# Plain fp32 for the first weight pieces of a two-block transformer kernel, and another order of its opening loads

## The reference

```
c_act = silu(c)                                   # c: 2048 numbers
mod   = c_act @ w_ada + b_ada                     # w_ada: 2048 x 12288
sh_m, sc_m, gt_m, sh_f, sc_f, gt_f = split(mod, 6)
h     = rmsnorm(x, pre_mix_norm) * (1 + sc_m) + sh_m
proj  = h @ w_in                                  # w_in: 2048 x 8208
```

## Time and profile before

| | |
|---|---|
| median of three executions | 2838.78 us |
| profiled execution: span, first to last instruction | 2835.2 us |
| the same execution's time outside its span | not shown by the profile; median minus span is 3.6 us |
| TensorE busy | 95% of the span, granted clock 0.980 of 2.4 GHz |
| VectorE busy | 68% |
| ScalarE busy | 45% |
| DMA over the span | 578.42 MB, 204 GB/s |
| the chain that ended last | TensorE 83%, VectorE 8%, DMA 5%, issue 2%, ScalarE 1% |

### The profile page before, as it was taken

The page is one execution under the profiler, slowest core; times in us unless marked ns, Lnnn a source line. Parts: engine busy times, 40 slices in busy tenths (PEclk is TensorE's granted clock), DMA queues, the critical chain, the costliest instruction groups (busy, mean ns, idle before and its releaser), DMA issues.

```text
span 2835.2 us, 35190 instructions
## 1 busy us (share of the span) xinstructions
PE 2696.8 (95%) x12829; PEld 2244.1 (79%) x12829; DVE 1937.8 (68%) x2165; ACT 1261.8 (45%) x1423; POOL 22.7 (1%) x12
## 2 busy tenths in 40 slices
PE   3699999999799999999989999999999999999998
PEld 3578878777688888888868788888888888888886
DVE  7979796987856666666675657555557666666667
ACT  2253453554444444444445454444444444444444
POOL 0000000000000000000000000000000000000000
PEclk8799999999999999999999999999999999999999
DMA  9968666567566666666646446665556666666664
GB/s 354 340 213 252 218 219 217 174 195 264 184 219 219 203 219 208 214 217 205 218 137 193 127 148 199 201 198 181 194 169 203 189 188 187 190 186 188 188 187 154
DMA packets 281266, 578.42 MB, mean 204 GB/s; under 512 B 19642, under 2 KB 20308, under 8 KB 280020
## 3 DMA queue, kind: packets, MB, share of 16 engines
q1 hardware_dynamic: 279060, 572.95, 63.1%
q10 hardware_dynamic: 2112, 4.19, 0.4%
HBM read 574.98 MB, written 2.10 MB: 204 GB/s over the span
## 4 chain that ended last, share of the span: by engine, by line
PE 83%; DVE 8%; DMA 5%; issue 2%; ACT 1%; SPq 0%; ACTq 0%; DVEq 0%
PE bank L450 25%; PE bank L451 25%; PE bank L455 25%; PE bank L708 4%; PE bank L705 3%; DMA ada_raw<-in_w_ada 2%; DMA early<-in_w_ada 2%; DVE w_lo L440 2%; DVE acc L1848 1%; DVE acc_w L1848 1%; DVE gd_t L2203 1%; PE bank L1113 0%; DVE gd_t L1817 0%; ACT w_hi L435 0%; DVE at_t L1817 0%
## 5 line engine op out<-in xcount | busy, mean ns | idle before, releaser
L440 DVE TENSOR_TENSOR w_lo<-raw,w_hi 128x1024 fp32r<-128x1024 f32 x880 | 1074.2, 1228 | 629.9 <-ACT w_hi L435 627.6
L435 ACT ACTIVATE w_hi<-raw 128x1024 fp32r<-128x1024 f32 x880 | 930.6, 1059 | 1254.2 <-PE bank L455 1118.9
L450 PE MATMUL bank<-w_hi,op_a_hi 128*128 128x512 f32 x2272 | 904.8, 398 | 34.1 <-DVE op_a_lo L1817 31.9
L451 PE MATMUL bank<-w_hi,op_a_lo 128*128 128x512 f32 x2272 | 890.7, 392 | 0.0
L455 PE MATMUL bank<-w_lo,op_a_hi 128*128 128x512 f32 x2272 | 610.6, 391 | 5.0 <-DVE w_lo L440 5.0
L450 PEld LDWEIGHTS bank<-w_hi,op_a_hi 128*128 128x128 f32 x2272 | 430.6, 190 | 125.2 <-DVE op_a_lo L1817 32.6
L455 PEld LDWEIGHTS bank<-w_lo,op_a_hi 128*128 128x128 f32 x2272 | 428.5, 189 | 95.8 <-DVE w_lo L440 5.8
L451 PEld LDWEIGHTS bank<-w_hi,op_a_lo 128*128 128x128 f32 x2272 | 430.7, 190 | 86.7 <-issue 1.0
L450 PE MATMUL bank<-w_hi,hid_hi 128*128 128x512 f32 x832 | 326.5, 392 | 0.0
L451 PE MATMUL bank<-w_hi,hid_lo 128*128 128x512 f32 x832 | 323.9, 389 | 0.0
L455 PE MATMUL bank<-w_lo,hid_hi 128*128 128x512 f32 x832 | 222.7, 389 | 0.0
(11 more groups left out here) (240 smaller groups left out, 1875.3 us busy)
## 6 DMA issues: line engine op xcount, KB each, us to landing
raw<-in_w_in SPq DMA_DIRECT2D x264, 512.0 KB, 4.6
raw<-in_w_ff SPq DMA_DIRECT2D x256, 512.0 KB, 3.7
raw<-in_ffn_w_up SPq DMA_DIRECT2D x176, 512.0 KB, 4.1
ada_raw<-in_w_ada SPq DMA_DIRECT2D x96, 512.0 KB, 5.3
raw<-in_ffn_w_down SPq DMA_DIRECT2D x88, 512.0 KB, 4.7
early<-in_w_ada SPq DMA_DIRECT2D x26, 1024.0 KB, 12.4
raw<-in_w_out SPq DMA_DIRECT2D x32, 512.0 KB, 4.8
ada_raw_f<-in_w_ada SPq DMA_DIRECT2D x32, 512.0 KB, 4.7
```

The costliest lines, as they stand in the source:

```text
L435: nc.scalar.activation(w_hi[:, gj % RAW], raw[:, j % RAW], ACT.Copy).then_inc(hi_ready, 1)
L440: nc.vector.tensor_tensor(w_lo[:, gj % RAW], raw[:, j % RAW], w_hi[:, gj % RAW].bitcast(F32), ALU.subtract).then_inc(lo_ready, 1)
L450: nc.tensor.matmul(where[:, t], hi(kt + k, tok), w_hi[:, s, k], start=first and k == 0, stop=False)
L451: nc.tensor.matmul(where[:, t], lo(kt + k, tok), w_hi[:, s, k], start=False, stop=False)
```

## The change

- Pieces 0 to 14 and piece 18 (`WHOLE`) are no longer split. TensorE multiplies them as they are, in plain float32, with the unsplit operand `X_T`: four products of 128x512 per piece (`whole_piece`). Such a step waits for the piece's landing and for `h32_ready`, or, for the first two rows of a quarter, for a new counter `xt_half` that VectorE raises when half of the quarter is modulated. Pieces 15, 16, 17 and everything from 19 on are split as before; `rounded(n)` counts only the split ones.
- SP loads only the unit matrix of the constants (64 KB) at first, then c alone, then blocks 4 and 5, then all other row vectors (14), then the remaining blocks with nothing between them. After block 31 come four small reads for the delta rule and the attention (`a_log`, `dt_b`, `sink`, `ab_raw`) and the rest of the constants, under one counter `rest_landed`.
- x is issued by ScalarE, behind blocks 0 to 3 and after its exponential for c_act. ScalarE also issues pieces 0 to 19 (`load_in(act, ...)`): 0 to 3 after each `X_T` copy, 4 to 9 after the first rounding, 10 to 15 after the second, 16 to 19 after the third, with the splits of 15, 16 and 17 between them.
- VectorE sums three pairs before it norms x. In the second and third quarter, half a pair of the next quarter stands ahead of the modulation. The bounds of the HGRN2 group (`bounds_open`, `bounds_done`) are made around pair 4 instead of at the start. The last pair is summed block by block (`add_last`).
- The decay stages begin at step 20 instead of 18; the delta-rule stages begin where they did.

```
+WHOLE = tuple(range(15)) + (18,)
-EARLY_LOADS = {7: range(0, 4), 11: range(4, 8), 17: (8, 9), 19: (10, 11), 25: (12, 13), 27: (14, 15), 29: (16,), 31: (17, 18, 19)}
...
+        def whole_piece(pe, n, kt, where, first, last):
+            raw_landed(pe, 0, n)
+            if kt % 4:
+                pe.wait_ge(h32_ready, kt // 4 + 1)
+            else:
+                pe.wait_ge(xt_half, kt // 4 + 1)
+            for k in range(PK):
+                for t in range(NT):
+                    mm = nc.tensor.matmul(where[:, t], X_T[:, kt + k, t * P:(t + 1) * P], raw[:, n % RAW, k],
+                                          start=first and k == 0, stop=last and k == PK - 1)
+            mm.then_inc(w_used, 1)
...
+        def load_in(eng, n):
+            m = n - RAW
+            if m in WHOLE:
+                eng.wait_ge(w_used, m + 1)
+            elif m >= 0:
+                eng.wait_ge(lo_ready, rounded(m))
+            load(eng, 0, n, win_piece(n))
...
-            sp.dma_start(table[:], consts).then_inc(loaded, 16)
+            sp.dma_start(ident, consts[:, C_ID:C_ID + P]).then_inc(loaded, 16)
...
-            sp.dma_start(X[:], x_in).then_inc(x_landed, 16)
...
+                if n == 31:
...
+                    sp.dma_start(table[:, P:], consts[:, P:]).then_inc(rest_landed, 16)
...
 (ScalarE)
+            nc.scalar.dma_start(X[:], x_in).then_inc(x_landed, 16)
...
                 f(X_T[:, 4 * q:4 * q + 4].rearrange("p k n -> p (k n)"), flat(n), ACT.Copy, xt_ready)
+                load_in(act, q)
...
-            for q in range(4):
-                for n in EARLY_SPLITS[q]:
-                    split_hi(act, 0, n, 0, n)
-                round_early(q)
...
+            round_early(0)
+            for n in range(RAW, 10):
+                load_in(act, n)
+            round_early(1)
+            for n in range(10, 16):
+                load_in(act, n)
+            round_early(2)
+            for n in range(EARLY_DONE - RAW, EARLY_DONE):
+                if n - 1 not in WHOLE:
+                    split_hi(act, 0, n - 1, 0, n - 1)
+                load_in(act, n)
+            for n in range(EARLY_DONE - 1, EARLY_DONE + 1):
+                split_hi(act, 0, n, 0, n)
+            round_early(3)
+            act.wait_ge(rest_landed, 80)
...
 (VectorE)
             add_early(0)
+            add_early(1)
+            add_early(2)
             newton(0)
             scaled_rows()
...
+            for q in range(1, 4):
+                add_early(4 * q + 1)
+                early_low(q - 1)
+                add_early(4 * q + 2)
+                if q < 3:
+                    add_early(4 * q + 3)
+                    add_early(4 * q + 4, (0, 1))
+                    early_operand(q)
+                    add_early(4 * q + 4, (2, 3))
+                else:
+                    early_split(*(n for n in range(12, 18) if n not in WHOLE))
+                    add_last(15)
+                    early_operand(3)
```

176 lines of the change are left out of this document (77 added, 99 removed).

## The result

The changed kernel is slower, by 0.26%: 2846.8 us (median of 9 runs, 2842.8 to 2849.9) against 2839.3 for the kernel before, measured beside it (9 runs, 2833.6 to 2844.1). The ratio is 1.0026, with a 95% interval of 1.0017 to 1.0034: about 7.5 us more where 5.8 less were forecast. The profiled execution has a span of 2845.8 us (2847.63 in all). Step 21, the marker of the prediction, starts at 164.78 us instead of 158.37, 6.4 later; forecast was 152.6. Up to 185 us little is added to that: TensorE's first pass over the delta-rule tables starts at 184.81 against 177.92, 6.9 later. The profiled spans differ by 10.6 us, though (2835.2 before), and the other 4 us do not lie in the opening: GpSimd's fill of `Y`, much further on, starts at 686.85 against 675.67, 11.2 later.

A forecast was written before the change was run, and what follows sets the result against it. TensorE's products bound the whole kernel; in the opening stage VectorE was late, data four us behind. Last sum 3.9 us earlier (most of 12.5 us removed splits becoming waits) plus tail 1.9: 2838.8 − 5.8 = 2833.0 us, range 2826 to 2839.

The forecast's parts named there:

- The opening: First stage, x behind block 3: pair 1 at about 20, x landing about 27, first modulation 46.5 against 46.74 us.
- 5.2 us of lost transfer: DMA queues before block 10 moves at 44.5 us: empty, then pieces of 1.35 us every 1.7, 4.3+0.9 us lost.
- The frame of VectorE: VectorE from first modulation to last sum: alone 76.0 us, ending 122.5; data later, block 29 at 119.0, last sum 133.2.
- split 17 is done at about 125, and VectorE wants it at 126.7: ScalarE's issue and split order for pieces 16 and 17, 5.5 us from issue to landing; every us beyond on the path.
- covered items: Costs taken as hidden: ScalarE's twenty issues in idle time, its tighter split order, the small reads, its wait for them.
- sums of the last pair 5.4: VectorE's pair 15 behind block 29, pair 14 (5.4) and three splits (3.4): 5.4 us, ending the last sum at 133.2.
- the tail of 19.4: Last sum to step 21: sums 2.0, steps 17 to 20 2.72, 3.6 and 5.44, narrow products 5.6; against 21.25 us.
- the third rival: TensorE runs whole pieces at half clock, 7.2 us each; VectorE waits 14 us in two quarters, about 2861 us; chance 0.05.
- piece 18 "is on the path": Step 18 in the tail: the whole piece takes 3.6 us against 2.72, 0.9 more, not covered.
- finds them landed: ScalarE's wait for the small reads at about 138 us, splits 21 and on behind it; reads land at about 134.
- the second: Splits were hidden by transfers; late x, split 17 or pieces lose 4 us, last sum 137, 2836.9 us; chance 0.30.
- What follows is unchanged: Everything after step 21 (152.6 us) stays the same and only comes earlier.

The follow-up runs named there:

- the run that undid it: Kernel with the three repairs, x back on SP's queue behind c and VectorE's norming of x behind pair 0: ratio 0.9988 to the kernel before.
- the three repairs: Changed kernel with piece 18 split again, pieces 16 to 18 issued ahead of ScalarE's splits, last pair's sums in turn: ratio 0.9981 to the kernel before.
- step 16 four times: Changed kernel with step 16's twelve products done four times: column sums and step 17 took 4.64 us together against 8.70.
- step 17 first: Changed kernel with step 17 run before the last quarter's column sums: step 21 stayed 26.40 us behind the last sum.

## Why the prediction was wrong

*The opening* came as worked out in the prediction: pair 1 at 20.02 (about 20), x's first square at 26.15 (27), the first X_T copy at 36.32 (37.1), the first modulation at 45.83 (46.5), the engines running down from 36 (164 GB/s from 36 to 40). The 5.2 us of lost transfer were 4.4 by the run that undid it. Two queues moved no more than one: 386 GB/s from 58 to 65 us with both in use, 387 in the earlier trace rows. The Trainium skill ("DMA: Bandwidth & Descriptors", section "Issuing engines are not separate DMA queues") says that transfers of several issuers run on the same 16 DMA engines, and the trace agrees.

*The frame of VectorE* held to 120.12 (119.0), with the 12.4 us of waits for blocks in it; the last of these (1.41) stands before pair 13, so that pair 14 started without a wait of its own for block 29. TensorE's 31.9 us of waits for the operand's low part are gone. A whole piece took 3.85 us in the first quarter (23.08 for six; 3.6 forecast), which began at half clock (0.50 from 47 to 50 us), covered as expected; at full clock it was 3.03 to 3.10 (step 18), so on the path it costs 0.3 to 0.4 us more than a split one and not 0.9.

*The first step that failed* is "split 17 is done at about 125, and VectorE wants it at 126.7". The mechanism was seen and priced ("every us beyond is on the path, at worst some 4"), but it stood among the covered items, on a landing of 5.5 us that no row ahead of the prediction shows. Two pieces that the kernel before issued at 122.8 and 123.9 had taken longer:

```profile
DMA to landing us min/median/max: 7.5/7.6/7.7
```

Here the two pieces took 8.0 and 7.3 us, one behind the other, the rounding ended at 130.9, and VectorE waited 3.13 us. Issuing ahead took 2.35 of that away, and with the three repairs VectorE made the three splits without a wait.

*The second* is "sums of the last pair 5.4". I read the new function for its order and not for its waits: in four sums into the same half each waits for the one before it, 0.80 us from start to start instead of 0.67. 0.9 us; in turn, they took 5.38.

*The third* is the tail of 19.4, which was 26.4, with 4.06 us of half clock in it and 3.1 of waiting. I weighed the clock where the change adds work (the whole pieces) and dropped it where the change takes work away. The fifteen whole pieces wait neither for a split nor for the operand's low part, so TensorE is done with them soon after their quarter is modulated. It had finished step 16 when the last pair's sums had hardly begun, stood idle for 6.2 us, and paid in the sums and in step 17. Before, TensorE was behind with its pieces all the way to the sums (step 16 ended at 137.4, and the granted clock was 1.00 from 130 to 140 us), and the clock was still up when the sums came. That is the third rival's mechanism in a place where the prediction did not look for it.

*The fourth* stood in two sentences that I took for harmless: piece 18 "is on the path" (0.9 us by the prediction, 0.4 measured) and ScalarE's wait for the small reads "finds them landed". Both hold. But a whole piece frees its buffer at another time, and what SP has behind that wait was not listed: piece 22, the `ada_raw` block, and on VectorE `ab_lo`. Splitting piece 18 took 3.65 us out of the tail, `ab_lo` alone 2.7.

In sum: 1.1 (pair 14 later than forecast) + 3.1 (split 17) + 0.9 (sums) + 4.1 (clock) + 3.1 (`ab_lo`) make 12.3 of the 12.2 us. That the two agree so well is in part chance: step 18 was 0.5 shorter than forecast, and steps 19 and 20 about as much longer. The first term was not tested by a run; the others were each taken away in one, the sums' only together with two others. Of the rivals, the second came nearest for the last sum ("split 17 or the pieces come late": 137, it was 138.4), but it left the tail's 1.9 us of gain standing. "What follows is unchanged" held to 185 us; beyond that the profile was 4 us later, less than this part varies between the runs, so it is neither borne out nor refuted.

The other half of the story is that little of the 12.5 us of VectorE's time was to be had, as the prediction said itself: VectorE waited 12.4 us for blocks instead. In the kernel with the three repairs the splits that remain are hidden by transfers too, and in the two runs that took such splits away the last sums started no earlier.

## What to carry to other kernels

When a change lets an engine free a buffer at another moment, list everything behind the wait on that buffer in the issuing queue, down to the last small transfer, and who needs it. When it removes work from TensorE's waiting time, ask what TensorE does in the stretch before the next short job: being busy right up to that job was here worth 4 us of clock. And if a term stands under "covered" with a margin of 1.7 us and a loss of 1 us per us beyond, it belongs in the sum, with the landing time taken from the longer end.

## What the runs showed of the hardware

What idle time before the column sums does to TensorE's clock is clear at its two ends. In the last quarter the 16 one-column products of the column sums took 1.84 to 1.95 us behind no idle time (before, and step 16 four times) and 3.57 behind 4.39 to 8.59 us of it (the changed kernel and six runs). The granted clock was 1.00 with step 16 four times and 0.50 in the changed kernel. The Trainium skill ("TensorE: Matmul & The Clock Gate", Part 1) holds the slow state for the default and activity for what releases it. These two ends agree with that.

Not expected was what lies between them. Behind 2.06 us the sums ran at full clock, behind 2.42 at half, and behind 2.73 mostly at half (3.24), which looks as if the length of the idle time decided. It does not alone: the second quarter's sums ran at full clock behind 3.47 us in the changed kernel and at half behind 2.56 in the run with step 17 first:

```profile
73.72 1.95 PE L730 MATMUL bank<-ones,acc 128*128 128x1 f32 x16 [3.47 <-DVE acc L1884]
...
73.70 3.57 PE L730 MATMUL bank<-ones,acc 128*128 128x1 f32 x16 [2.56 <-DVE acc L1884]
```

Nor does the sums' own clock settle the next step: with the three repairs the sums ran at full clock and the second half of step 17 behind them at half (0.63 us a product from 137.64 on). The narrow products took 5.4 us behind a wait of 3.09 in the changed kernel, and 7.0 to 7.2 behind 2.73 to 2.96 in four other runs. What decides these was not tried, so a gain that rests on an idle stretch of two to three and a half microseconds, as that of the three repairs does in part, should not be counted on.

In these traces a sum on VectorE (128x512) that waits for the one right before it starts 0.80 us after it; where each waits only for the one before that, it is 0.67.
